# A transformer layer on one core: orders of work at the two SwiGLU beginnings and in the attention units

## What is computed

```python
x = x + 0.5 * swiglu_ffn(rms_norm(x, ffn1_norm_g), w_gate, w_up, w_down)     # SwiGLU 1
h = rms_norm(x, mix_norm_g); proj = h @ w_in                                 # seven groups of 512 columns
# 8 heads x 64: q and k normed per head, each 64-frame chunk attends to 9 chunks, plus a bias
scores = einsum('bqhd,bkhd->bhqk', qc, kb) * scale + bias; p = softmax(scores); out = p @ v
# 4 heads x 128: gated linear recurrence (HGRN2), normed and gated
x = x + concat(attn_out, hgrn_out) @ w_out
x = x + 0.5 * swiglu_ffn(rms_norm(x, ffn2_norm_g), ...)                      # SwiGLU 2
```

## Time and profile before

| | |
|---|---|
| median of 3 executions | 1950.54 us (1948.69 to 1952.28) |
| the profiled execution | 1952.53 us |
| its span, first to last instruction | 1951.0 us |
| mean granted TensorE clock | 0.992 of full speed |
| TensorE busy | 1902.4 us, 98% of the span |
| VectorE, ScalarE, GpSimd busy | 57%, 35%, 22% |

### The profile page before, as it was taken

One profiled execution on the slowest core, in us unless ns is written; L12 is line 12 of the kernel. 1 busy time (PEld: TensorE's weight loads), 2 busy tenths in 40 slices (PEclk: granted clock), 3 DMA queues, 4 the chain that ended last, 5 costly groups with the idle time before them and its releaser, 6 DMA issues.

```text
span 1951.0 us, 24682 instructions
## 1 busy us (share of the span) xinstructions
PE 1902.4 (98%) x9384; PEld 1577.1 (81%) x9384; DVE 1105.9 (57%) x1491; ACT 674.5 (35%) x1027; POOL 420.8 (22%) x322
## 2 busy tenths in 40 slices
PE   8899999999999999999999889999999999999999
PEld 7788888888888888888888567877888888888887
DVE  5866666665555630244455764357666666655564
ACT  6323323323333533220223563254232332234332
POOL 2322332241102110002221320002322432231030
PEclk9999999999999999999999899999999999999999
DMA  4444435446866443323332510044354535358663
GB/s 165 146 165 155 170 132 184 146 145 235 319 194 193 129 146 118 105 68 116 129 119 85 183 58 1 22 130 144 126 173 146 178 135 182 136 200 334 216 193 141
DMA packets 220364, 295.77 MB, mean 152 GB/s; under 512 B 14544, under 2 KB 117080, under 8 KB 220256
## 3 DMA queue, kind: packets, MB, share of 16 engines
q1 hardware_dynamic: 206752, 262.19, 39.7%
q0 software_dynamic: 5152, 16.85, 2.7%
q10 hardware_dynamic: 8352, 15.27, 2.0%
HBM read 205.37 MB, written 91.51 MB: 152 GB/s over the span
## 4 chain that ended last, share of the span: by engine, by line
PE 92%; DVE 3%; ACT 2%; issue 2%; DMA 1%; SPq 0%; POOL 0%; DVEq 0%; ACTq 0%; POOLq 0%
PE ps L699 28%; PE ps L701 28%; PE ps L700 28%; PE ps L900 2%; PE ps L985 1%; PE ps L998 1%; PE ps L733 1%; PE ps L1016 1%; DMA raw<-ffn_w_up 1%; DVE wlo L1635 0%; DVE S L1976 0%; PE ps L921 0%; ACT PT L1465 0%; PE ps L891 0%; PE ps L924 0%
## 5 line engine op out<-in xcount | busy, mean ns | idle before, releaser
L699 PE MATMUL ps<-hThi,whi 128*128 128x512 f32 x896 | 351.1, 392 | 4.4 <-ACT xs L1175 2.8
L700 PE MATMUL ps<-hTlo,whi 128*128 128x512 f32 x896 | 349.5, 390 | 0.0
L701 PE MATMUL ps<-hThi,wlo 128*128 128x512 f32 x896 | 349.3, 390 | 0.0
L699 PE MATMUL ps<-whi 128*128 128x512 f32 x616 | 240.1, 390 | 1.0 <-DVE wlo L1717 1.0
L700 PE MATMUL ps<-wlo,whi 128*128 128x512 f32 x616 | 239.7, 389 | 0.0
L701 PE MATMUL ps<-whi,wlo 128*128 128x512 f32 x616 | 239.6, 389 | 0.0
L699 PEld LDWEIGHTS ps<-hThi,whi 128*128 128x128 f32 x896 | 169.1, 189 | 39.6 <-issue 4.7
L699 PE MATMUL ps<-hXhi,whi 128*128 128x512 f32 x480 | 188.9, 394 | 11.4 <-DVE wlo L1635 11.4
L700 PEld LDWEIGHTS ps<-hTlo,whi 128*128 128x128 f32 x896 | 169.1, 189 | 35.0
L701 PEld LDWEIGHTS ps<-hThi,wlo 128*128 128x128 f32 x896 | 168.7, 188 | 35.2
L701 PE MATMUL ps<-hXhi,wlo 128*128 128x512 f32 x480 | 188.6, 393 | 0.0
(11 more groups left out here) (192 smaller groups left out, 2924.7 us busy)
## 6 DMA issues: line engine op xcount, KB each, us to landing
hid_scratch<-hid SPq DMA_DIRECT2D x132, 256.0 KB, 3.2
raw<-ffn_w_gate SPq DMA_DIRECT2D x44, 512.0 KB, 3.7
raw<-ffn_w_up SPq DMA_DIRECT2D x44, 512.0 KB, 4.9
wdb<-ffn_w_down SPq DMA_DIRECT2D x44, 512.0 KB, 4.0
wd_scratch<-wdb SPq DMA_DIRECT2D x88, 256.0 KB, 4.5
raw<-hid_scratch SPq DMA_DIRECT2D x80, 256.0 KB, 2.7
rawx<-hid_scratch SPq DMA_DIRECT2D x74, 256.0 KB, 2.8
raw<-w_in SPq DMA_DIRECT2D x28, 512.0 KB, 5.0
```

The source lines that it names most:

```text
L699: pe.matmul(dst, ahi, bhi, start=first, stop=False, skip_group_check=onto)
L700: pe.matmul(dst, ahi, blo, start=False, stop=False, skip_group_check=onto)
L701: return pe.matmul(dst, alo, bhi, start=False, stop=last, skip_group_check=onto)
```

## The change

It reorders work and moves no arithmetic between engines.

1. First SwiGLU: TensorE does one more product (product 2) ahead of the turns of tiles 4 to 7, so that each of these stands one product later in its list. ScalarE makes the hi parts of tiles 1 and 2 ahead of weight 0, and spreads the squares of tiles 4 to 7 among its other work, where they stood together behind weight 5. VectorE makes the lo part of tile 2 ahead of weight 0 and norms tiles 4 to 7 between the weights.
2. Both SwiGLUs: `PREPARED_AFTER` spreads weights 11 to 18 over products 15 to 19, so that weight 14, and with it the four sums, comes after product 17 and behind the addition of L1682.
3. Attention: ScalarE copies an even turned unit ahead of the exponential of the unit two further on, where the copy came after it. The square of k and both norms come one unit later. Unit 3 uses bank 6 as unit 1 does, so that step 1 no longer waits for `ro_ready` (step 2 does), and `values(0)` waits for the maximum of unit 3.
4. Second SwiGLU: ScalarE does `keep_turned` of tile 5 and weights 2 and 3 ahead of the square of tile 7.

```diff
-PREPARED_AFTER = {12: [8], 13: [9], 14: [10], 15: [11, 12], 16: [13, 14, 15]}
+PREPARED_AFTER = {12: [8], 13: [9], 14: [10], 15: [11], 16: [12, 13], 17: [14], 18: [15, 16], 19: [17, 18]}
...
-    if n <= 16:
+    if n <= 19:
         return PREPARED_AFTER.get(n, [])
...
-SQUARE_AT, SUM_AT, NORM_AT = (1, 3), (3, 5), (5, 7)
+SQUARE_AT, SUM_AT, NORM_AT = (1, 4), (3, 5), (6, 8)
...
-            return 6 if v == 1 else 2 * ((v + 1) % 2)
+            return 6 if v in (1, 3) else 2 * ((v + 1) % 2)
...
             early_turn(3, 1)
+            products(0, 2, 3)
             for t in range(4, TT):
-                products(0, t - 2, t - 1)
+                products(0, t - 1, t)
                 turn_tile(R_FFN1, t)
-            products(0, 6, SEQ)
+            products(0, 7, SEQ)
...
-                if w == 1:
+                if w == 2:
                     pe.wait_ge(ro_ready, HH + 1)
...
                 if w:
                     pe.wait_ge(outT_ready, 2 * w)
+                else:
+                    pe.wait_ge(unit_max, 4)
...
+            early_hi_part(1, 0)
+            early_hi_part(2, 0)
             weight_hi(0, 0)
-            for t in range(1, 4):
-                early_hi_part(t, 0)
+            early_hi_part(3, 0)
             weight_hi(0, 1)
...
             weight_hi(0, 2)
+            square(R_FFN1, 4)
+            square(R_FFN1, 5)
             early_hi_part(0, 1)
...
             early_keep(1, 1)
+            square(R_FFN1, 6)
             early_hi_part(2, 1)
...
             early_keep(3, 1)
+            square(R_FFN1, 7)
             weight_hi(0, 5)
-            for t in range(4, TT):
-                square(R_FFN1, t)
...
+            def take_turned(v):
+
+                act.wait_ge(unit_turned, v + 1)
+                if v >= SLOTS:
+                    act.wait_ge(unit_out, v + 1 - SLOTS)
+                act.activation(PT[:, v % SLOTS, :], ps[:, 4 * HALF:4 * HALF + BAND], ACT.Copy)\
+                   .then_inc(PT_by_scalar, 1)
...
             for v in range(NV + 4):
+                scalar_takes = 2 <= v < NV + 2 and by_scalar(v - 2)
+                if scalar_takes and v % 2 == 0:
+                    take_turned(v - 2)
                 if v < NV:
...
+                if scalar_takes and v % 2:
+                    take_turned(v - 2)
...
             weight_hi(1, 1)
+            keep_turned(R_FFN2, TT - 3)
+            weight_hi(1, 2)
+            weight_hi(1, 3)
             square(R_FFN2, TT - 1)
-            keep_turned(R_FFN2, TT - 3)
-            for w in range(2, 6):
-                weight_hi(1, w)
+            weight_hi(1, 4)
+            weight_hi(1, 5)
...
             early_lo_part(1, 0)
+            early_lo_part(2, 0)
             weight_lo(0, 0)
-            early_lo_part(2, 0)
             early_lo_part(3, 0)
...
+            normalise(R_FFN1, 4)
             weight_lo(0, 3)
+            normalise(R_FFN1, 5)
             early_lo_part(2, 1)
             early_lo_part(3, 1)
-            for t in range(4, TT):
-                weight_lo(0, t)
-                normalise(R_FFN1, t)
+            weight_lo(0, 4)
+            normalise(R_FFN1, 6)
+            weight_lo(0, 5)
+            normalise(R_FFN1, 7)
+            weight_lo(0, 6)
+            weight_lo(0, 7)
```

## The result

The changed kernel takes 1930.56 us (median of 4 executions, 1928.37 to 1931.81) against 1950.47 for the kernel before, a ratio of 0.9897 (0.988 to 0.9914): 19.9 us faster. The forecast was 30.8 us faster, 1919.7, in a range of 1914.2 to 1929.0, so the sign was right and the size was not. The profiled execution took 1928.37 us, its span 1926.8.

What follows compares the result with a forecast made beforehand. TensorE was taken as the bound, busy 98%, so only its gaps and lower-clock time could be won. First SwiGLU 12.0, second 12.4 and attention 6.4 sum to 30.8 off 1950.54: 1919.7 us, range 1914.2 to 1929.0.

Steps and rivals of the forecast that it cites:

- Up to product 8: First SwiGLU's start: earlier product 0, no gap ahead of tile 4's turn and full clock save 5.8 us.
- Product 16: First SwiGLU: VectorE's chain starts only 3.2 us earlier, so product 16 gets a new wait of 1.6 us.
- rival D: Both SwiGLUs: product 19 waits for the lo weight named in the bracket, so its waits stay; 1935.3 us, chance 0.06.
- rival E: Later SwiGLU tiles: VectorE meets GpSimd more and TensorE waits 1.2 us in each of 38 tiles; 1965 us, chance 0.04.
- What is late next is up1: First SwiGLU: VectorE's remaining work ends up1 at 84.9, so product 22 waits 1.7 us; bounds 0 and 3.9.
- its copy in the second SwiGLU: Second SwiGLU: up1 is ready as product 22 wants it, so 0 us comes back; bounds 0 and 2.2.
- The low clock in the first SwiGLU's first 100 us: Sign of being wrong: a low clock in either SwiGLU's first 100 us; the forecast had it only in attention step 1.
- rival C: Both SwiGLUs: two more VectorE meetings with GpSimd in each, and a clock fall in the first; 1925.8 us, chance 0.18.
- the forecast's 6.4: Attention: the new bank, copies and norms save 2.0, 1.6, 1.6 and 1.2 us over four pairs, 6.4 in all.
- the bank: Attention step 1: with unit 3 in bank 6 it no longer waits for the scaling, saving 1.15 us.
- the bound of 2.2: Attention step 1: upper bound, in us, of the gain if the clock stayed up; the forecast took 0.
- rival B: Attention: TensorE's clock stays up in step 1; 1917.5 us, chance 0.18.

Runs made afterwards that it cites:

- stores first: The changed kernel with the fifth tile's weight loads and the second down-projection load issued behind the hidden stores in both SwiGLUs: 1922.81 us, 0.9851 of the kernel before.
- weights alone: The kernel before with only the new `PREPARED_AFTER` and its bound (point 2 of the change): 1946.11 us, 0.9974 of the kernel before.
- one load alone: The changed kernel with only the fifth tile's gate and up weight loads moved behind the hidden stores: 1928.04 us, 0.9887 of the kernel before.
- bank undone: The changed kernel with unit 3 back in bank 0 and step 1 waiting for `ro_ready` again: 1933.29 us, 0.9915 of the kernel before.
- copies and norms alone: Two runs on the kernel before: only even units' copies ahead of exponentials, 1946.89 us (0.9975); only square of k and norms one unit later, 1949.06 us (0.9988).

## Why the forecast was too high

**Right.** Up to product 8 the walk held: product 0 started at 16.30 (forecast 16.4), tile 4's turn at 29.10 without a wait, tile 7's at 39.94 (40.0). Product 16 waited 1.32 (1.6), product 19 started at 75.20 (75.2) without a wait. So it was `u2` that held product 19 and not the lo weight in the bracket, and rival D is out. Product 0 of the second SwiGLU follows straight behind tile 6's turn, and nothing waits past product 30, so rival E is out too.

**The step that failed** is "What is late next is up1: VectorE still has ..., a wait of 1.7", with its bounds of 0 to 3.9, and its copy in the second SwiGLU (0, bounds 0 and 2.2). It priced what VectorE has to do ahead of `up1` and left out what `up1` waits for besides: the landing of a store, issued by SyncE behind 2 MB of loads and 3.6 us of other stores. The first wait came out at 5.92 and the second at 2.09. In the first SwiGLU that is 4.2 us more of waiting, and 2.8 us of the clock that the forecast had given back: 7.0 of the 7.3 missing. In the second it is 2.1 of the 2.3. The low clock in the first SwiGLU's first 100 us is a sign of being wrong that the prediction had named. The stores first and the weights alone show it: move the store and the waits shrink, leave it and they come back. In four places where VectorE stood idle with "issue" (both SwiGLUs of after, the first of the weights alone and of one load alone) `up1` starts 0.1 to 0.2 us behind that store's landing. VectorE's own part of the term, once the store was out of the way, measured 2.27 for the 1.7. The working of that part doesn't add up as it is written: six operations of 1.75, four of 0.68 and those from PSUM take over 14 us, which from `u2` at 75 ends past 89 and not at 84.9. It gives about 85 only if the count begins with weights 12 and 13, near 71. Counted so, the stores first had five full meetings with GpSimd and one in part, for the six of the forecast. Even that wait brought the lower clock in the profile, so the stores first reach product 24 at 93.14, 9.4 us earlier than before and not 12.0: 1.7 of the 2.6 that is left is the clock, which the forecast had falling only behind a wait of over 2.85 (rival C).

**Rival C** named the right place and a time of 1925.8 but not the cause: two more meetings with GpSimd. In the changed kernel VectorE stood idle for 4.68 us there.

**Attention.** At the clock of before, the forecast's 6.4 measured 5.5: the copies and the norms 4.7, the bank 0.8 of 1.15. With the clock up it is 9.3: the clock gives 3.8 more and not the bound of 2.2. The prediction had the 3.8 as TensorE's work and expected VectorE's chain to leave 2.2 of it; the chain kept nothing back. Pairs two and three are 29.20 apart where they were 30.5, 1.3 shorter and not 1.6, and the turns still wait 1.7 for ScalarE's copies and not 1.0. The forecast chose the clock of step 1 as down, with 0.18 for up (rival B). Neither is a property of the changed kernel: the gap ahead of step 1 is 1.74 behind one of 1.36, and the clock was up in three of the five profiles with it, lower for a shorter time in one and down as before in one. The executions of the stores first differ likewise: spans of 1918.8 and 1919.3 at a mean clock of 1.000, and of 1923.2 and 1923.5 at 0.996. The last of these is the profiled one, with the lower clock in two places, behind product 22's wait (1.7 us) and in attention (3.8); a mean of 1.000 leaves room for neither. The four of after had spans of 1926.8, 1928.4, 1930.2 and 1929.6 at 0.998, 0.997, 0.996 and 0.996, so its profile is the fastest of four and that of before is slower than its median; each makes about half of what the profiled pair saves beyond the medians. With the low clock in attention the table's sum would be 24.1 - 3.8 = 20.3 (an estimate), near the median's 19.9. That the three slower executions had it in attention is likely but argued only: they have no profile.

**Left open.** Why the clock falls behind the same gap in one execution and not in the next; why before's profile was slower than its median; and the 1.3 us of product 16, which nothing here tried.

## To carry to other kernels

Before a wait is priced as gone, take the instruction that is late next and list all its waits, buffer reuse with them, then follow a store's wait back through the whole queue that issues it: a long wait on one engine can hide late transfers, and removing it brings them up at the next use. An idle engine with "issue" as its releaser and a wait on a landing in the code is a place to look. Stores that free a buffer belong ahead of loads that have time, and a load's arrival also decides when the engine that works on it gets in another's way.

## What the runs showed of the hardware

- The granted clock of TensorE behind one and the same pair of gaps (1.36 and 1.74 us) was at the upper level in some executions and at the lower one in others, up to 10.2 us long and up to 3.8 us in cost. Behind gaps of 1.36 and 2.97 (before, the weights alone, bank undone, copies and norms alone) it fell each time, in seven profiles. Behind a single gap ahead of product 22 it stayed up after 2.09 us (after, second SwiGLU) and fell after 2.27 (stores first), 3.81 and 3.88 (one load alone), 4.13 (weights alone) and 5.92 (after). The Trainium skill (TensorE: Matmul & The Clock Gate, section What's actually happening) says that the slow start of one kernel differs from run to run; the four executions of the stores first show the same for the middle of a kernel, two at 1.000 and two at 0.996, 4.3 us apart.
- VectorE's additions of two SBUF tiles of 128x512 took 0.67 to 0.69 alone and up to 1.81, mostly 1.74 to 1.78, where they met a GpSimd addition in full; many that met one in part took 1.15 to 1.19. The Trainium skill (SBUF — State Buffer, section Who interferes with whom) calls the port pair of these two engines an exclusive lock; the rows agree that one holds up the other, by at most about 1.1 us, where GpSimd's additions took 1.26 to 1.78.
- Two stores of 256 KB each held SyncE's queue for 3.62 us in the first SwiGLU of the changed kernel, with two weight loads just in front of them, 2.54 in the stores first and 0.90 in both SwiGLUs of one load alone. The same two loads in front gave 1.36 in the changed kernel's second SwiGLU. So the time that a row of the queue takes to issue doesn't follow from what it moves alone; what sets it was not tested.
- The same store of 256 KB landed 3.7 us after its issue with the stores first, 4.5 in the first SwiGLU of the changed kernel and 5.8 with one load alone.
